# A two-block transformer kernel on one core: the dilated attention of the even layer with its tokens in parity order, and one gate block computed first

## What is computed

```python
DIL_PAIRS = ((128, 1), (512, 4), (2048, 16))

def ssd_dilated_layer(x, ...):
    proj = jnp.einsum("bsd,df->bsf", rms_norm_2(x, norm_w), w_in)
    z, xbc, dt, q, k, v, g = split_cols(proj, EVEN_IN_SIZES)
    xbc = jax.nn.silu(causal_dwconv(xbc, conv_w, conv_b))
    ...
    y = ssd_chunked_scan(xs, dt, A, bm, cm) + d_skip[:, None] * xs
    y = rms_norm_2(y * jax.nn.silu(z), ssd_norm_w)
    q = partial_rope_2(rms_norm_2(q, q_norm), pos)
    k = partial_rope_2(rms_norm_2(k, k_norm), pos)
    for gi, (window, dil) in enumerate(DIL_PAIRS):
        o_g, lse_g = dilated_group(q[hs], k[hs], v[hs], window, dil)
    wts = jax.nn.softmax(jnp.stack(lses, axis=0), axis=0)
    o = jnp.sum(wts[..., None] * jnp.stack(outs, axis=0), axis=0)
    o = o * jax.nn.silu(g)
    return x + jnp.einsum("bsf,fd->bsd", jnp.concatenate([y, o], axis=-1), w_out)
```

## Time and profile before

| | |
|---|---|
| Median of 3 runs | 1759.93 us (1755.76 to 1761.22) |
| The profiled execution, its own time | 1758.77 us |
| Its span in the profile | 1756.9 us |
| PE busy | 1715.1 us, 98% |
| DVE busy | 1260.3 us, 72% |
| ACT busy | 964.7 us, 55% |
| Mean share of the 16 DMA engines in the span | about half in most slices |

### The profile page before, as it was taken

How to read it: one execution, slowest core, us unless ns; L and a number is a source line. 1 busy time by engine, 2 the same in 40 slices (tenths; PEclk the granted TensorE clock), 3 DMA queues, 4 the chain that set the end, 5 groups by cost and what they waited for, 6 DMA issues and landing times. The chain is left out here.

```text
span 1756.9 us, 28519 instructions
## 1 busy us (share of the span) xinstructions
PE 1715.1 (98%) x10554; PEld 1487.3 (85%) x10554; DVE 1260.3 (72%) x2362; ACT 964.7 (55%) x1630; POOL 22.7 (1%) x21
## 2 busy tenths in 40 slices
PE   7999999999999999999999999999999999899998
PEld 6888899998888888888899988788889878767887
DVE  6666777567876667666876577766677896886775
ACT  5444554665554446444645565544556556563474
POOL 1000000000000000000000000000000000000000
PEclk9999999999999999999999999999999999999999
DMA  8545555634545454554556435454554544204531
GB/s 316 185 180 200 193 192 180 237 135 183 192 185 196 179 216 156 193 201 179 200 197 232 171 125 205 161 209 179 191 201 173 189 155 169 108 1 144 204 120 60
DMA packets 29906, 311.66 MB, mean 177 GB/s; under 512 B 3312, under 2 KB 3696, under 8 KB 4848
## 3 DMA queue, kind: packets, MB, share of 16 engines
q1 hardware_dynamic: 28944, 307.18, 47.1%
q0 software_dynamic: 864, 3.15, 0.5%
HBM read 309.26 MB, written 1.05 MB: 177 GB/s over the span
## 5 line engine op out<-in xcount | busy, mean ns | idle before, releaser
L502 ACT ACTIVATE region_r<-ring 128x1024 fp32r<-128x1024 f32 x505 | 525.0, 1054 | 358.3 <-PE psum L914 333.4
L508 DVE TENSOR_TENSOR ring_r<-ring,region_r 128x1024 fp32r<-128x1024 f32 x496 | 592.3, 1220 | 130.6 <-ACT region_r L502 125.3
L914 PE MATMUL psum<-xs_r,region_r 128*128 128x256 f32 (+2 forms) x3160 | 581.2, 331 | 3.3 <-ACT region_r L502 1.7
L914 PEld LDWEIGHTS psum<-xs_r,region_r 128*128 128x128 f32 (+1 forms) x3160 | 467.4, 188 | 66.0 <-issue 7.8
L914 PE MATMUL psum<-region_r 128*128 128x512 f32 (+3 forms) x1056 | 330.6, 381 | 0.0
L914 PE MATMUL psum<-xs_r,ring_r 128*128 128x256 f32 x2344 | 317.5, 278 | 0.0
L914 PEld LDWEIGHTS psum<-xs_r,ring_r 128*128 128x128 f32 x2344 | 303.8, 188 | 15.8
L914 PE MATMUL psum<-region_r,xs_r 128*128 128x512 f32 (+2 forms) x1056 | 270.3, 349 | 6.2 <-DVE region L2755 3.1
L914 PEld LDWEIGHTS psum<-region_r 128*128 128x128 f32 (+2 forms) x1056 | 193.1, 185 | 36.2 <-DVE region_r L2433 0.6
L914 PEld LDWEIGHTS psum<-region_r,xs_r 128*128 128x128 f32 x1056 | 182.6, 188 | 35.9 <-ACT xs_r L1855 4.5
L914 PE MATMUL psum<-ring_r,region_r 128*128 128x512 f32 (+1 forms) x472 | 169.5, 375 | 0.0
(11 more groups left out here) (250 smaller groups left out, 1558.7 us busy)
## 6 DMA issues: line engine op xcount, KB each, us to landing
ring<-in_weights SPq DMA_DIRECT2D x192, 1536.0 KB, 6.4
gpost<-in_posts POOLq DMA_DIRECT2D x6, 512.0 KB, 4.5
cst<-in_const SPq DMA_DIRECT2D x1, 1213.0 KB, 22.7
PTs<-in_mem SPq DMA_DIRECT2D x1, 1024.0 KB, 5.6
x<-in_x SPq DMA_DIRECT2D x1, 1024.0 KB, 8.0
out<-x SPq DMA_DIRECT2D x2, 512.0 KB, 2.6
pars<-in_par SPq DMA_DIRECT2D x1, 368.0 KB, 6.1
p<-in_par SPq DMA_DIRECT2D x1, 206.0 KB, 22.8
```

The costliest lines, as they stand in the source:

```text
L502: eng.activation(unit.high, unit.like_high(unit.raw), ACT.Copy).then_inc(h_ready, 1)
L508: eng.tensor_tensor(unit.like_high(unit.low), unit.like_high(unit.raw), unit.high.bitcast(F32), ALU.subtract)\
L914: ins = pe.matmul(bank, lhsT, rhs, start=start, stop=stop)
```

## The change

**Tokens in parity order.** For q, k, v the stationary operand becomes a view of the same input with a step of two: tile 0 is the even tokens, tile 1 the odd ones (`hH_parity`, `hL_parity`, blocks 0 to 8). The gate blocks 9 and 10 keep the natural order. The tables of the rotation get a copy in parity order. Since 4 and 16 are even, a token of groups 1 and 2 sees only tokens of its own parity: of the 256 by 256 scores of these groups only the two 128 by 128 blocks on the diagonal are left. Group 0 needs all 256 keys for both tiles.

**Two banks of 512.** A unit's scores are now 256 columns of group 0 and 128 of each of the other groups for each tile of queries: 1024 columns in two full banks, where there were 1152 in three uses of a bank. One bank holds group 0 ("near"), the other the two dilated groups ("far"). DVE reads both banks with one instruction for each query tile, 512 columns wide, straight to one maximum. There are 8 turns in place of 9, two copies of 512 in place of three of 384. `HEAD_PAIR` lays the heads of two units so that group 0 stands in one half of the partitions and groups 1 and 2 in the other.

**Order of the blocks.** Block 9 is first, in place of block 0. Each of the blocks 0, 1, 2 then follows four xbc tiles, and after the last four comes "dt". Blocks 3 to 7 follow as before, then block 10, with no block 9 between. The numbers of `EVEN_STEPS` go up by four.

**Output.** `even_out` puts the outputs back in natural order while it reads them: it reads the bank with a step of 128 columns between neighbours.

```diff
-    order = block(0) + tiles("xbc", range(0, 5)) + block(1) + tiles("xbc", range(5, 10)) + block(2)
-    order += tiles("xbc", range(10, 16)) + [("dt",)]
-    for c in (3, 4, 5, 6, 7, 9, 10):
+    order = block(9)
+    for c in range(3):
+        order += tiles("xbc", range(4 * c, 4 * c + 4)) + block(c)
+    order += tiles("xbc", range(12, 16)) + [("dt",)]
+    for c in (3, 4, 5, 6, 7, 10):
         order += block(c)
...
+HEAD_PAIR = [(0, 0), (0, 1), (1, 1), (0, 2), (1, 2), (1, 0)]
...
+        hH_parity, hL_parity = (low_high_r[:, :, c:c + NT, :].rearrange("p k c t -> p k (c t)")
+                                .rearrange("p k (n i) -> p i k n", i=NT) for c in (NT, 0))
...
+                        near, far = (Job("S", tag, s, b) for b in range(2))
+                        near.wait_empty(pe)
+                        far.wait_empty(pe)
+                        for i in range(NT):
+                            at = i * SEQ
+                            last = i == NT - 1
+                            mm(far.bank[:, at:at + P], q_of(s, 1)[:, i, :], k_of(s, 1)[:, i, :], True, True)
+                            mm(near.bank[:, at:at + SEQ].rearrange("p (i t) -> p i t", i=NT), q_of(s, 0)[:, i, :], k_of(s, 0),
+                               True, True, near.full if last else None)
+                            mm(far.bank[:, at + P:at + SEQ], q_of(s, 2)[:, i, :], k_of(s, 2)[:, i, :], True, True,
+                               far.full if last else None)
...
+                        for n in range(NT):
+                            todo.append((job.bank[half, 0:SEQ].rearrange("p (i n) -> p i n", i=NT), v_of(s, 0)[n], pt[:, :, n, :]))
+                        for b in (1, 2):
+                            for i in range(NT):
+                                todo.append((job.bank[half, i * P:(i + 1) * P], v_of(s, b)[i], pt[:, i, 1 + b, :]))
...
-            even_block(9)
...
+                        both = psum[:, jobs[0].at:jobs[1].at + 1, :]
+                        for job in jobs:
+                            job.wait_full(dve)
+                        for i in range(NT):
+                            own(dve.memset(small[:, 64 + 2 * s + i:65 + 2 * s + i], 0.0))
+                            ins = dve.tensor_tensor_reduce(pairs_of(scores_of(kind, s, i * 512, (i + 1) * 512)),
+                                                           both[:, :, i * SEQ:(i + 1) * SEQ],
+                                                           pairs_of(C("dil")[:, i * 512:(i + 1) * 512]),
+                                                           1.0, NEG, ALU.add, ALU.max, m[:, i:i + 1])
...
-                        own(dve.tensor_reduce(m[:, 0:2], m[:, 0:6].rearrange("p (i b) -> p i b", i=NT), AX.X, ALU.max))
-                        own.settle()
...
-            EVEN_STEPS = {("squares", 0, 0): 34, ("squares", 0, 1): 36, ("normed", 0, 0): 38, ("normed", 0, 1): 40,
-                          ("squares", 1, 0): 48, ("squares", 1, 1): 50, ("normed", 1, 0): 52, ("normed", 1, 1): 55}
+            EVEN_STEPS = {("squares", 0, 0): 38, ("squares", 0, 1): 40, ("normed", 0, 0): 42, ("normed", 0, 1): 44,
+                          ("squares", 1, 0): 52, ("squares", 1, 1): 54, ("normed", 1, 0): 56, ("normed", 1, 1): 59}
...
-                dve.tensor_tensor(even_mixedT[rows, 8 + h // 2, :], job.bank[rows, 0:SEQ], egT[rows, h // 2, :],
-                                  ALU.mult).then_inc(job.free, 1)
+                dve.tensor_tensor(even_mixedT[rows, 8 + h // 2, :].rearrange("p (n two) -> p n two", two=NT),
+                                  job.bank[rows, 0:SEQ].rearrange("p (two n) -> p n two", two=NT),
+                                  egT[rows, h // 2, :].rearrange("p (n two) -> p n two", two=NT), ALU.mult)\
+                    .then_inc(job.free, 1)
```

More of the change, by code:

```diff
@@ L329, in tail_jobs @@
         j.add("G", "xbc", t)
-    for c in range(11):
+    for c in (9, *range(8), 10):
         for i in range(NT):
-            if c != 8:
-                j.add("Y", "eb", c, i)
+            j.add("Y", "eb", c, i)
     for name in ("dt", "dtT"):
@@ L806, in prob_tiles @@
             elif kind == "dil":
[L807 removed]
+                at = [b * 512 + n * P for n in range(4)]
             else:
@@ L1191, in scores @@
                         return
-                    if kind == "dil" and 0 in branches:
-                        jobs = [Job("S", tag, s, b) for b in range(2)]
-                        for job in jobs:
-                            job.wait_empty(pe)
-                        for n in range(NT):
-                            for b, job in enumerate(jobs):
-                                to = job.bank[:, n * P:P + n * SEQ]
-                                if n:
-                                    to = to.rearrange("p (i t) -> p i t", i=NT)
-                                mm(to, q_of(s, b)[:, n, :], k_of(s, b) if n else k_of(s, b)[:, 0, :], True, True,
-                                   job.full if n else None)
+                    if kind == "dil":
+                        if not branches:
+                            return
+                        near, far = (Job("S", tag, s, b) for b in range(2))
[9 more added lines that the diff above has]
+                               far.full if last else None)
                         return
@@ L1509, in project_rows, with token_block @@
                             used.append(w_used[(first + n) // 3 % SLOTS])
-            def token_block(name, c, u, last, weave=lambda j: None):
+            def token_block(name, c, u, last, weave=lambda j: None, parts=(hH, hL)):
                 jobs = [Job(name, c, i) for i in range(NT)]
@@ L1520, in token_block @@
                             job.wait_empty(pe)
-                        products(job.bank, [h[:, i, kk, :] for h in (hH, hL)],
+                        products(job.bank, [h[:, i, kk, :] for h in parts],
                                  [w[:, kk % 2 * 512:(kk % 2 + 1) * 512] for w in (unit.high, unit.low)],
@@ L1673, in last_rows @@
                         job.wait_empty(pe)
-                    products(job.bank, [h[:, i, kk, :] for h in (hH, hL)],
+                    products(job.bank, [h[:, i, kk, :] for h in (hH_parity, hL_parity)],
                              [w[:, kk % 2 * 512:(kk % 2 + 1) * 512] for w in (unit.high, unit.low)],
@@ L1967, in evacuate @@
                                 Job("PV", tag, output_of(units, s - 2)).wait_full(act_)
-                        n = 512 if kind == "mem" else 384
-                        copy(job, PTs[:, s % 2, b * 384:b * 384 + n], job.bank[:, 0:n])
+                        n = 512 if kind in ("mem", "dil") else 384
+                        copy(job, PTs[:, s % 2, b * n:(b + 1) * n], job.bank[:, 0:n])
                 for s in range(len(units) + LAG[tag]):
@@ L2501, in front @@
                         Job("PT", tag, s - n, BRANCHES[units[s - n][0]] - 1).wait_full(dve)
-                    for b in range(BRANCHES[kind]):
+                    if kind == "dil":
+                        jobs = [Job("S", tag, s, b) for b in range(2)]
+                        both = psum[:, jobs[0].at:jobs[1].at + 1, :]
+                        for job in jobs:
+                            job.wait_full(dve)
+                        for i in range(NT):
+                            own(dve.memset(small[:, 64 + 2 * s + i:65 + 2 * s + i], 0.0))
[3 more added lines that the diff above has]
+                                                           1.0, NEG, ALU.add, ALU.max, m[:, i:i + 1])
+                            if i:
+                                ins.then_inc(jobs[0].free, 1)
+                            else:
+                                own(ins)
+                        jobs[0].wait_emptied(dve)
+                        dve.memset(small[:, 52:53], 0.0).then_inc(jobs[1].free, 1)
+                    for b in range(BRANCHES[kind] if kind != "dil" else 0):
                         job = Job("S", tag, s, b)
@@ L3251, in constants @@
     c = {
-        "ident": np.eye(P), "causal": added(causal), "dil0": added(causal & (t - s <= 128)),
-        "dil1": added(causal & ((t - s) % 4 == 0)), "dil2": added(causal & ((t - s) % 16 == 0)),
-    }
+        "ident": np.eye(P), "causal": added(causal),
+    }
+    near, fours, sixteens = (causal & ok for ok in (t - s <= 128, (t - s) % 4 == 0, (t - s) % 16 == 0))
+    seen = [np.concatenate([near[i::2, 0::2], near[i::2, 1::2], fours[i::2, i::2], sixteens[i::2, i::2]], 1)
+            for i in range(NT)]
+    assert not any(far[i::2, 1 - i::2].any() for far in (fours, sixteens) for i in range(NT))
+    c["dil"] = np.where(np.concatenate(seen, 1), 0.0, NEG)
     reach = causal.T.astype(float)
```

117 lines of the change are left out of this document (52 added, 65 removed).

## The result

The changed kernel takes 1748.16 us (median of 5 runs, 1744.93 to 1749.01), the kernel before 1758.77 us beside it (1755.76 to 1761.22). The ratio is 0.9936 with a 95% interval of 0.9921 to 0.9951: faster by 0.64%, 10.6 us. The forecast was 1746, with a range of 1741 to 1754. The profiled execution of the changed kernel took 1747.27 us, its span is 1745.2 us.

What follows compares the result with a forecast made beforehand. PE, busy 98% of the span, was taken as the bound, with DVE the longer chain in the new attention. Terms -15.5 + 2.2 = -13.3 us took the profiled 1758.8 to 1745.5; forecast 1746, range 1741 to 1754.

Steps and rivals of the forecast that it cites:

- Attention, -15.5: Even layer's attention: two banks shorten the stage from 54.8 to 39.3 us, with DVE the longer chain.
- The last term, 1.4 us: Attention: 1.4 us added because DVE and PE, both 3.95 us a step, would now and then wait for each other.
- The low clock, taken as gone: Attention: the 3.4 us at half clock was taken as gone; if it came back it would cost 1.7 us.
- Block 9 first, +2.2: Projection: k made 10.98 us later against 8.8 us of slack, so PE waits for DVE in block 10, +2.2 us.
- Strided weights, 0: Blocks 0 to 8: 432 loads with a step of 8 bytes stay hidden behind matmuls of 229 ns, 0 us.
- Two of the prediction's own signs of being wrong: Projection: weight loads of blocks 0 to 8 longer than block 9's, and PE's blocks over 11 us.
- The rival with loads three times as long, 1794 us: Blocks 0 to 8: strided loads outlast the matmuls; at three times, 1794 us; strided loads' chance 0.10.
- The output's read, 0: Attention's collections: DVE reading PSUM with a step of 128 columns costs 0, at most 1.6 us.
- Sum, -13.3: Whole kernel: -15.5 + 2.2 = -13.3 us, from the profiled 1758.8 to 1745.5.
- No pairing: Attention scores: far matmuls don't run beside the near one, PE's step 4.8 us, total 1751.5; chance 0.07.
- Handoffs stay: Attention: DVE's gaps come from PE's order of turns, not three branches; about 6 us stay, 1752; chance 0.12.

Runs made afterwards that it cites:

- e6: Changed kernel with each collection of an attention output on DVE done twice; 1753.46 us, one run.
- e9: The changed kernel measured again, unchanged, as base for later runs on the same chip; 1747.63 us.
- e1: Changed kernel with blocks 0 to 8 loading their tokens contiguously instead of with a step of 8 bytes; 1747.55 us.
- e4: Kernel before with only the new order of the blocks (block 9 first); 1762.09 us, ratio 1.0019 to the kernel before.
- e12: Changed kernel with the outputs read from PSUM contiguously, without the step of 128 columns; 1749.16 us, one run.
- e5: Changed kernel with HEAD_PAIR reordered so all three groups of a head number stand in the same half of the partitions; 1762.96 us, one run.
- e8: Changed kernel with k's rotation sooner, the scan output's two squares moved to GpSimd and the last scaling in two halves; 1745.88 us.
- e11: Changed kernel with k's rotation sooner, sum of squares and last scaling each in two halves, low parts reordered, squares left off GpSimd; 1745.53 us.
- e2: Changed kernel with the step of 8 bytes in block 1 alone, the other eight blocks loading contiguously; 1747.24 us, one run.
- e7: Changed kernel with one score matmul of 128 columns done twice in each of the eight attention steps; 1747.77 us, one run.
- e3: Changed kernel with one number changed (56 to 54), so two low parts stand behind k's second rotation on DVE; 1748.05 us.
- e10: e3 measured again, beside its base e9 on one chip; 1746.23 us.

## Why the prediction was right, and where its terms were off

The time came out in the range and 2.2 us above the forecast. A part of that nearness is luck: against the kernel before, the forecast was -13.9 us and the measurement -10.6, but the kernel before itself came out 1.2 us lower when it was measured beside the changed one. The terms:

- **Attention, -15.5.** Measured -15.0, B 39.8 for 39.3. The mechanism is as predicted: DVE is the longer chain (e6). It starts 1.3 us after the first scores and has 37.0 us of work, where the prediction had 1.3 and 36.6. PE's step was predicted with 3.95 and is 3.99; its parts 1.1, 1.0 and 1.86 are 1.09, 1.02 and 1.88. DVE's full step, also 3.95, is 4.02. The read of 512 columns on DVE came out at the 0.62 us that the step from 128 to 256 gave. The last term, 1.4 us for the times when the two wait for each other, is right by luck: after the first scores DVE has no pause over 0.1 us, and its 1.5 us of idle time are some thirty short ones between its own instructions.
- **The low clock, taken as gone.** It is gone from B in every two-bank, paired kernel but e6. In the profiled execution it came back in A, right behind the new wait, +1.7 us. The prediction had named that price and left it out of the sum. In e9, the same program, it isn't behind that wait.
- **Block 9 first, +2.2.** Measured 1.87 us, and 2.2 to 2.3 where the blocks are not slow (e1, e4): the 8.8 us of slack and the 10.98 us of shift were read correctly. What went uncounted is that it brings the low clock with it in some executions, so that the order alone cost 3.3 us in the median (e4).
- **Strided weights, 0.** Measured +2.0 us in A, 2.3 of PE's time. This is the term that was mis-sized, and its reasoning fell with it. It was that a load hidden behind a matmul of 229 ns can't show, and that it takes 260 ns to matter. With stepped loads the loads last 195 ns on average for 188, still well below 229, and yet the matmuls start 233 ns apart, and 118 ns apart in the tiles behind them for 113.5. Two of the prediction's own signs of being wrong are there: loads longer than those of block 9, and blocks over 11 us (11.20). The Trainium skill's rule (page "SBUF — State Buffer", section "Door 1: The DMA port swizzle") that such a step keeps the full rate is nearly what is measured, 2% off in the matmuls and 4% in the loads. The rival with loads three times as long, 1794 us, is excluded.
- **The output's read, 0.** Confirmed by e12. The rule on neighbouring pairs in PSUM (the Trainium skill, page "Advanced Engine Details and Errata", section "Memory Cachelines") speaks of matmuls; for DVE's read, where the prediction put up to 1.6 us beside it, no cost is measured.
- **Sum, -13.3.** The stretches give -15.0 + 1.9 + 1.7 + 2.3 - 0.1 = -9.2 us. The 1.7 are the low clock of the one execution that was profiled; without it the change is worth -10.9 us by the stretches, as the medians have it with 10.6. The two profiled executions differ by 11.5, of which some 2.5 us come from ahead of the even layer, where nothing was changed. So the forecast was 2.4 us too good on the change itself, and 4 in an execution where the clock falls behind the wait.
- **Rivals.** "No pairing" had the right price for a step (4.8 us forecast, 4.85 in e5), but its 1751.5 us took the full clock for granted; without pairing the one execution took 1763, longer than the kernel before. "Handoffs stay" would have needed steps over 4.6 us.

## What to carry to other kernels

When two chains of a pipeline have nearly the same length, don't compare their steps: look which engine never waits for the other. Here DVE waits once and PE for 4.5 us, and 2.7 us more on DVE lengthen the stage by 2.7, 1.8 us more on PE by 0.55. A relief of the longer chain is worth only what the other one leaves, here about a microsecond (e8), and work that is moved behind the end of a stage can be missing there (e11: 2.0 us gained in B, 1.2 lost in C). When a step is moved later on an engine that has slack, look at once for work on it that is not yet needed and can stand behind the moved step; here one number was worth most of the wait. And judge edits of 1 or 2 us by stretches between fixed events of the trace, since the median of five runs hides them.

## What the runs showed of the hardware that was not expected

- With loads of 128 stationary columns at a step of 8 bytes, matmuls of 512 columns start 233 ns apart in place of 229. The slower rhythm lasts through later contiguous loads (tiles of 256 columns at 117.7 ns for 113.5, a whole contiguous block at 233 in e2) and then ends between two matmuls. The kernel before, with no stepped load, has it too for 14 us. The cause is open.
- The low clock, 0.50 for 3.4 us, came right behind the wait for k in the changed kernel, e1, e2 and e4, not in e5, e6, e7, e9 and e12, and never there where the wait is missing (before, e3, e8, e10, e11). The four waits that it followed are the longest (1.87, 2.21, 2.23 and 2.32 us), the five others 1.83 to 1.86; but the changed kernel and e9 are the same program with 1.87 and 1.86, and it also came behind e6's wait of 1.70 us and e9's of 1.22, so the length of the wait alone doesn't decide it.
- With the score matmuls of a head all in one half of the rows the clock was at 0.50 for 23.9 us while PE was busy throughout; with the halves paired it was at 1.00 over the same stretch of the program (e5, one execution, against the other changed kernels).
- GpSimd multiplied 128x1024 fp32 numbers in 1.89 us, where DVE takes 1.22; while it did, a scaling of two columns on DVE took 0.60 us in place of 0.17 (e8, both times).
- VectorE reads PSUM with a step of 128 columns between neighbours as fast as plainly, 419 and 420 ns for 64x256.
